# Reordering exponentials, casts and row norms in a hybrid pooling and HGRN2 decoder step

## The chip, the cores and the metric

The kernel runs on the 8 cores of one Trainium2 chip. Each core takes one prompt of 2048 tokens, with the 16 meta tokens ahead of it, and 16 of the 128 sample tokens; no core waits for another. The metric is the device time of the slowest core in microseconds (us), the median of several runs.

## The reference, cut to what matters

```python
h = rmsnorm(x, g_mix)
u, q, f, v, og, ga, gb = split(h @ w_in)      # 4 x 512, 512, then 2 x 1024 columns
# branch A: trailing means over 2, 4, 8, 16 positions, minus the token
ya = (group_map(pool_mean(u) - u) * pool_scale) @ w_a
# branch B: gated linear recurrence, 4 heads, dk = dv = 128
f = lb + (1 - lb) * sigmoid(f);  k = 1 - f
S_t = diag(f_t) S_{t-1} + outer(k_t, v_t);  o_t = S_t^T silu(q_t)
yb = (rmsnorm(o, g_onorm) * silu(og)) @ w_b
x = x + (sigmoid(ga) * ya + sigmoid(gb) * yb) @ w_out
x = x + square(relu(rmsnorm(x, g_mlp) @ w_up)) @ w_down
y = rmsnorm(x, g_final)
```

16 learned meta tokens stand ahead of every prompt and are dropped from y. The last 15 rows of u and the last state S are outputs too.

## The kernel before

The 2048 prompt rows are worked in four groups of 512 (four row tiles of 128). The first stage, `group(g)` for g = 0 to 3, computes everything up to the projection by w_out, with h held transposed (channels on partitions) in `hT[g % 2]`. Group 0 carries the 32 sample and meta rows as well, so its tiles are 544 columns wide where those of the other groups have 512. A tile of 544 columns takes two PSUM banks, one of 512 takes one; `banks` hands out banks 0 to 3 in turn. The second stage, `up(g)` and `down(g)`, is the MLP; the change doesn't touch it.

The order of the work is made by a planner, `Timeline`. `U(fn)` emits a unit, a product that fills one PSUM tile and its eviction, and moves the planner's time t on by 1 (by 0.5 for the products by w_a and w_b, by 2 for the first one by w_out). `tl.at(t, fn)` and `tl.later(dt, fn)` put side work on a list, which is emitted, earliest due time first, after the unit with which t reaches it. Times in the code are thus counted in units, and they set only the place in each engine's queue. Every engine works through its queue in order and waits with semaphores that `Prog` works out from the buffers; DMAs are issued in the queues of SyncE (SP) and of GpSimd (POOL, the weights).

A group runs: four units of f (`u_f`, sigmoid); four of v (`u_v`), four of u (`u_u`) and four of q (`u_q`, silu), in group 0 in that order with a small v unit for the meta and sample rows first, in the others mixed; four of og; then gb, ga with the product by w_a (`u_ya`), the product by w_b (`u_yb`) with the rest of gb; and w_out. ScalarE (ACT) evicts f, v, u, q, og, ga and gb.

Side work, each with its due time counted from `b0`, the end of the f units:

- `prep_ln`, `prep_scan`, `prep_exp`, `prep_k`, `prep_D`, `prep_E`, per head: log of f on ScalarE, running sum on VectorE (DVE), two exponentials on ScalarE (`prep_exp`, which writes one of the two buffers `T3`), the scaled k on VectorE (`prep_k`, which reads `T3`), decay factors. `prep_q(m)` (VectorE) follows each q unit by 1.5.
- `meta_state` (group 0): four transposes of k, their copy by ScalarE, four products into the state, their copy by ScalarE. `state_scale(0)` (VectorE) scales the state, `state_cast` (ScalarE) casts it to bf16 for the products.
- `r_tile(g, t)`: the recurrence on 128 tokens in six steps: `a` (transposes of k and the score product, lines 739 to 749, which read all four heads of k and q), `o` (lines 758 to 765), `n1`, a cast, `n2`, and `p` (transposes of the normed output, then ScalarE's copy into `obT`, which the products by w_b read).
- `pool_u`: running means of each u unit, on VectorE; a scan (line 812) where the window is 8 or 16.
- `rms1` norms one row tile of the next group: ScalarE squares and sums into the bf16 buffer `xn[j]` (two in turn), POOL makes the factor, `scaled` multiplies the rows by it into the same buffer, `fin` transposes them into the next `hT`. `fin` has two forms: eight TensorE transposes and a VectorE eviction that multiplies by g_mix (lines 617 and 572), or, with `dmat`, a DMA transpose issued by SP (line 653), after which `scale_rows` (line 868) multiplies by g_mix in eight VectorE operations for the group. Before, group 0 norms the rows of group 1 in the first form, groups 1 and 2 those of their successors in the second. The rows are loaded into three buffers `xr` in turn, which the residual rows (`xload`, `xslice`) use as well.
- `mk`, `scaled`, `evict`, `warm`: the same norm for group 0's own rows at the start, where `start` (the last argument of `rms1`) puts the multiplication on VectorE, with filler matmuls between.
- `more` (group 0): the blocks of w_in and the other weights, loaded from POOL's queue, where the copies of `prep_exp` stand too (line 686).

## Time and profile before

| what | value |
|---|---|
| median of 3 runs | 917.6 us (917.01 to 918.33) |
| the profiled execution's own time | 917.9 us |
| its span on the slowest core, core 7 | 916.4 us |
| spans of the eight cores | 914.6 to 916.4 us |
| mean granted TensorE clock, core 7 | 0.997 |
| group 0, first matmul of f to that of group 1 | 20.9 to 145.6 us |
| groups 1 and 2 | 145.6 to 249.5 us, 249.5 to 353.4 us |
| group 3 with its last products, then the MLP | to about 458 us, to 916.4 us |

The page counts busy time over the span of one execution. In 40 slices of 22.9 us the busy tenths of TensorE are 9 in all but the first two (4 and 8) and the last (7):

```profile
PE   4889999999999999999999999999999999999997
```

A line of a timeline begins with start and length in us; a group of equal instructions in a row is one line with xN, and the bracket at its end is how long the engine had been idle and which engine and line ended that. Idle time of an engine that nobody waits for costs nothing, so the waits of TensorE are read first.

### The profile page before, as it was taken

The page shows a single profiled execution, that of the slowest core. Times are in us where ns is not written, and L with a number is a line of the kernel's source. Part 1 is how long each engine was busy: PE and PEld are TensorE (multiplying, and loading weights), DVE is VectorE, ACT ScalarE, POOL GpSimd, SP SyncE. Part 2 cuts the span into 40 slices and gives each one's busy share as a digit, 9 for nine tenths or more (in the row PEclk, how much of TensorE's full clock was granted, in tenths as well). Part 3 has the DMA queues.
Part 4 walks back from the last instruction along what each step waited for, and adds up shares of the span by engine and source line. Part 5 has one row for each costly group of instructions (what it writes and reads, how often), then busy time and mean ns, then how long its engine had stood idle before and what let it go on. Part 6 is the DMA issues. An engine that isn't in the chain of part 4 may idle for free.

```text
span 916.4 us, 15069 instructions; the slowest of 8 cores (914.6 to 916.4 us)
## 1 busy us (share of the span) xinstructions
PE 877.8 (96%) x5017; PEld 453.6 (49%) x5017; DVE 419.5 (46%) x692; ACT 360.7 (39%) x636; POOL 120.2 (13%) x190
## 2 busy tenths in 40 slices
PE   4889999999999999999999999999999999999997
PEld 3556654454444444455444444444444444688443
DVE  4654563866657665854543222442143411333122
ACT  4634445566274645552233322332223321333222
POOL 3112330144101530243110000000000000000000
PEclk9999999999999999999999999999999999999999
DMA  9999724138604377996999341300520002200011
GB/s 175 164 169 197 138 79 161 44 107 181 194 28 116 104 173 209 176 140 88 188 210 194 62 125 61 93 1 2 137 70 23 1 20 73 73 1 1 31 64 70
DMA packets 81480, 94.90 MB, mean 104 GB/s; under 512 B 27741, under 2 KB 62173, under 8 KB 81388
## 3 DMA queue, kind: packets, MB, share of 16 engines
q1 hardware_dynamic: 57420, 63.52, 23.8%
q0 software_dynamic: 23984, 30.41, 23.5%
q8 instruction: 42, 0.69, 0.3%
q14 instruction: 34, 0.28, 0.1%
HBM read 92.35 MB, written 26.11 MB: 129 GB/s over the span
## 4 chain that ended last, share of the span: by engine, by line
PE 84%; DVE 5%; ACT 4%; issue 4%; POOL 1%; DMA 1%; DVEq 0%; SPq 0%; ACTq 0%; POOLq 0%
PE ps L591 46%; PE ps L1328 24%; PE ps L603 8%; ACT arena L569 4%; PE ps L1034 2%; DVE arena L572 1%; DVE arena L672 1%; POOL arena L572 1%; DMA arena<-meta 1%; DVE arena L692 0%; PE ps L748 0%; PE ps L1326 0%; PE ps L765 0%; PE ps L617 0%; PE ps L1217 0%
## 5 line engine op out<-in xcount | busy, mean ns | idle before, releaser
L591 PE MATMUL ps<-arena 128*128 128x512 bf16 (+2 forms) x2720 | 494.0, 338 | 10.4 <-ACT arena L569 7.6
L591 PEld LDWEIGHTS ps<-arena 128*128 128x128 bf16 x2720 | 259.8, 98 | 217.0 <-issue 23.6
L569 ACT ACTIVATE arena<-ps 128x512 f32<-128x512 f32 (+7 forms) x328 | 190.8, 598 | 292.4 <-PE ps L591 216.5
L569 ACT ACTIVATE arena<-arena 128x1024 bf16<-128x1024 f32 (+7 forms) x235 | 154.5, 670 | 256.3 <-DVE arena L1342 167.3
L1328 PE MATMUL ps<-arena 128*128 128x512 bf16 x1024 | 222.0, 379 | 0.0
L572 DVE TENSOR_TENSOR arena<-arena 128x512 bf16<-128x512 f32 (+6 forms) x214 | 146.2, 689 | 137.4 <-ACT arena L569 129.0
L1328 PEld LDWEIGHTS ps<-arena 128*128 128x128 bf16 x1024 | 100.0, 98 | 121.4 <-issue 1.3
L572 DVE TENSOR_TENSOR arena<-ps,arena 128x512 f32<-128x512 f32 (+5 forms) x155 | 107.9, 714 | 82.3 <-PE ps L591 26.1
L603 PE MATMUL ps<-arena 128*128 128x512 bf16 (+2 forms) x480 | 109.2, 383 | 0.0
L1342 DVE SCALAR_TENSOR_TENSOR arena<-ps,arena 128x1024 f32<-128x1024 f32 (+2 forms) x18 | 22.0, 1223 | 152.0 <-PE ps L1328 137.4
L572 POOL TENSOR_TENSOR arena<-arena 128x512 f32<-128x512 bf16 (+7 forms) x78 | 75.5, 975 | 73.4 <-DMA arena<-sth 27.1
L603 PEld LDWEIGHTS ps<-arena 128*128 128x128 bf16 (+2 forms) x480 | 46.3, 98 | 57.3 <-issue 3.9
L1351 DVE SCALAR_TENSOR_TENSOR arena<-arena 128x1024 f32<-128x1024 f32 (+2 forms) x18 | 22.0, 1224 | 34.2 <-ACT arena L569 34.2
L672 DVE TENSOR_TENSOR_SCAN arena<-arena 128x512 f32<-128x512 bf16 (+1 forms) x16 | 19.6, 1227 | 22.3 <-ACT arena L569 22.3
L686 POOL COPY arena<-arena 128x4 f32<-128x4 f32 x16 | 7.0, 438 | 96.7 <-ACT arena L569 96.7
L617 PE MATMUL ps<-arena 128*128 128x128 bf16 (+1 forms) x72 | 6.9, 255 | 12.0 <-DVE arena L647 11.0
L868 DVE TENSOR_SCALAR arena<-arena 128x512 bf16<-128x512 bf16 (+1 forms) x48 | 16.8, 350 | 3.1 <-DVE arena L868 0.9
L572 DVE TENSOR_TENSOR ps<-ps,arena 128x512 f32<-128x512 f32 x16 | 11.1, 695 | 10.4 <-PE ps L886 10.4
L752 DVE CAST_PREDICATED arena<-arena,ps 128x512 bf16<-128x512 uint32 x16 | 11.0, 687 | 8.5 <-PE ps L749 8.5
L1034 PE MATMUL ps<-arena 128*128 128x512 bf16 x64 | 14.5, 379 | 0.0
L748 PE MATMUL ps<-arena 128*64 128x128 bf16 x64 | 6.5, 223 | 7.3 <-ACT arena L569 4.5
L617 PEld LDWEIGHTS ps<-arena 128*128 128x128 bf16 (+1 forms) x72 | 5.7, 118 | 14.8 <-issue 14.3
(97 smaller groups left out, 259.2 us busy)
## 6 DMA issues: line engine op xcount, KB each, us to landing
arena<-xp SPq DMA_DIRECT2D x32, 512.0 KB, 5.4
arena<-w_in POOLq DMA_DIRECT2D x9, 1024.0 KB, 20.6
x1d<-arena SPq DMA_DIRECT2D x16, 512.0 KB, 5.2
arena<-w_up POOLq DMA_DIRECT2D x8, 1024.0 KB, 12.8
arena<-x1d SPq DMA_DIRECT2D x16, 512.0 KB, 3.8
y_p<-arena SPq DMA_DIRECT2D x15, 512.0 KB, 2.9
arena<-w_down POOLq DMA_DIRECT2D x5, 1024.0 KB, 23.7
h2d<-arena SPq DMA_DIRECT2D x16, 256.0 KB, 4.9
```

What stands on the lines that cost most here:

```text
L569: P.add("act", lambda h: h.activation(out=out, in_=in_, func=func, **kw), reads=reads, writes=writes)
L572: P.add(eng, lambda h: h.tensor_tensor(out=out, in0=a, in1=b, op=op), reads=reads, writes=writes)
L591: i = h.matmul(ps[:, bb, 0:m], lhsT=wfn(k), rhs=rfn(k, c, m), start=(k == 0), stop=(k == K - 1))
L603: i = h.matmul(ps[0:rows, b, :], lhsT=lfn(k), rhs=rfn(k), start=(k == 0), stop=(k == K - 1))
L617: i = h.transpose(out=o[:, k, 0:rows], in_=src[0:rows, k * 128:(k + 1) * 128], identity=ident_b[0:rows, 0:rows])
L672: P.add("dve", lambda h: h.tensor_tensor_scan(out=t2[:, c:544], data0=smask[:, c - 16:528], data1=t2[:, c:544], initial=0.0, op0=ALU.mult, ...
L752: P.add("dve", lambda h: h.copy_predicated(out=AT[i], mask=tri.bitcast(U32).unsqueeze(1).to_broadcast([128, 4, 128]), data=pA), reads=[b_p ...
L868: P.add("dve", lambda h: h.tensor_scalar(out=X[:, k, 0:n], in0=X[:, k, 0:n], scalar1=w[:, k:k + 1], scalar2=None, op0=ALU.mult), reads=buf ...
L1034: i = h.matmul(ps[:, b + half, :], lhsT=mT[:, k, 0:128], rhs=wo[:, k, half * 512:(half + 1) * 512], start=(k == 0), stop=(k == 7))
L1328: x = h.matmul(ps[0:rows, b + half, :], lhsT=aT[:, f, c:c + rows], rhs=rhs, start=(f == 0), stop=(f == 31))
L1342: P.add("dve", lambda h: h.scalar_tensor_tensor(out=sl, in0=src, scalar=s_(2), in1=sl, op0=ALU.mult, op1=ALU.add), reads=bsrc + [bst] + bx ...
L1351: P.add("dve", lambda h, c0=c0, c1=c1: h.scalar_tensor_tensor(out=xi[0:rows, c0:c1], in0=xi[0:rows, c0:c1], scalar=s_(5), in1=gfin[0:rows, ...
```

## The change

It touches the planner's due times and one form, not the arithmetic apart from where g_mix is multiplied in for group 1:

- `prep_exp` and `prep_k` of group 0 go from due times 2, 3, 4, 6 after `b0` to 2, 4, 6, 7 (the planner's e = 1 is in these), `prep_E` to 8; those of the other groups stay.
- `meta_state` is cut in two; the product and its copy come 1.1 later.
- the first `state_cast` of each group goes from 10 to 13.2 after `b0` (2 more in group 0).
- pooling of u units 2 and 3 of group 0: due 1.4 to 1.9 later.
- rows of group 1: normed in group 0 from due time 10 after the og units rather than 12, transposed by DMA, scaled by `scale_rows`; in all groups `scaled` comes 2.4 after the square rather than 1.6, `fin` 3.6 after it rather than 3.1. Row loads move with them.
- start: row tile 2 is multiplied on VectorE rather than ScalarE, and after the eviction of tile 1.

```diff
@@ -711,13 +711,15 @@
             tt(E, D1, D2[:, :, 0:4], ALU.mult, [b_D1, b_D2], [b_E])
             P.add("dve", lambda h: h.tensor_copy(out=D2[:, :, 0:1], in_=D2[:, :, 4:5]), reads=[b_D2], writes=[b_D2])
 
-        def meta_state():
+        def meta_1():
             def tr(h):
                 for k in range(4):
                     i = h.transpose(out=psT[0:32, k, :], in_=kt[:, k, 0:32], identity=ident_b)
                 return i
             P.add("pe", tr, reads=r_kt.bufs + [b_idb], writes=[b_pT[0]])
             act(ktT[1][0:32], psT[0:32, 0:4, :], AF.Copy, [b_pT[0]], r_ktT[1].bufs)
+
+        def meta_2():
 
             def mu(h):
                 for k in range(4):
@@ -818,7 +820,7 @@
                 if g == 0:
                     P.add("dve", lambda h: h.tensor_copy(out=u_s[:, gg, :], in_=u[:, 0:16]), reads=bu, writes=[b_us])
                 P.add("dve", lambda h: h.tensor_copy(out=hist[:, gg, :], in_=u[:, 528:544]), reads=bu, writes=[b_hist])
-            a, b = (((5.0, 5.0), (4.6, 4.6), (5.1, 6.1), (6.2, 7.2)) if g == 0 else ((4.9, 4.9), (3.4, 3.5), (5.5, 6.5), (4.6, 5.6)))[gg]
+            a, b = (((5.0, 5.0), (4.6, 4.6), (7.0, 8.0), (7.6, 8.6)) if g == 0 else ((4.9, 4.9), (3.4, 3.5), (5.5, 6.5), (4.6, 5.6)))[gg]
             for op in first + mid:
                 tl.later(a, op)
             tl.later(b, fin)
@@ -1065,7 +1067,7 @@
                 early = {}
                 A(19.5, load_rest2)
                 for t in range(3):
-                    A(20.1 + t, lambda t=t: ([activate(r) for r in r_x[1:3]] if t == 0 else None, early.update({t: xload(x_rows(1, t), 128, r_wa.bufs)})))
+                    A(21.1 + 0.3 * t, lambda t=t: ([activate(r) for r in r_x[1:3]] if t == 0 else None, early.update({t: xload(x_rows(1, t), 128, r_wa.bufs)})))
                 A(24.1, lambda: [fold_wa2(gg) for gg in range(4)])
                 A(27.0, sample_pool)
                 A(36.0, fold_wb)
@@ -1100,17 +1102,19 @@
             def B(t, fn):
                 tl.at(b0 + t, fn)
             e = 1 if g == 0 else 0
+            x0_, x1_, x2_, x3_ = (2, 4, 6, 7) if g == 0 else (1, 2, 3, 5)
             B(0, lambda: ([prep_ln(g, i) for i in range(4)], prep_scan(g, 0), prep_scan(g, 1)))
-            B(1 + e, lambda: (prep_exp(g, 0), prep_scan(g, 2), prep_k(g, 0)))
-            B(2 + e, lambda: (prep_exp(g, 1), prep_scan(g, 3), prep_k(g, 1)))
-            B(3 + e, lambda: (prep_exp(g, 2), prep_k(g, 2)))
-            B(5 + e, lambda: (prep_exp(g, 3), prep_k(g, 3), prep_D(g)))
-            B(6 + e, lambda: prep_E(g))
+            B(x0_, lambda: (prep_exp(g, 0), prep_scan(g, 2), prep_k(g, 0)))
+            B(x1_, lambda: (prep_exp(g, 1), prep_scan(g, 3), prep_k(g, 1)))
+            B(x2_, lambda: (prep_exp(g, 2), prep_k(g, 2)))
+            B(x3_, lambda: (prep_exp(g, 3), prep_k(g, 3), prep_D(g)))
+            B(x3_ + 1, lambda: prep_E(g))
             e = 2 if g == 0 else 0
             if g == 0:
-                B(9, meta_state)
+                B(9, meta_1)
+                B(10.1, meta_2)
             B(9 + e, lambda: ([activate(r) for r in r_sogr], state_scale(0)))
-            B(10 + e, state_cast)
+            B(13.2 + e, state_cast)
             rs = [r_tile(g, t) for t in range(4)]
             for t in range(4):
                 z = 15.6 + e + 3.35 * t
@@ -1141,18 +1145,17 @@
 
                 def pre(t):
                     i = xl[t]
-                    rfin.append(rms1(xr[i], r_x[i].bufs, 128, t, N[:, :, 128 * t:128 * t + 128], bN[t], g > 0))
-                for t, z in enumerate((0, 1, 2, 14 if g == 0 else 9)):
+                    rfin.append(rms1(xr[i], r_x[i].bufs, 128, t, N[:, :, 128 * t:128 * t + 128], bN[t], True))
+                for t, z in enumerate((0, 1, 2, 13 if g == 0 else 9.5)):
                     if g > 0 or t == 3:
                         tl.later(z, lambda t=t: xl.update({t: xload(x_rows(g + 1, t), 128)}))
-                for t, z in enumerate((12, 16, 19, 22) if g == 0 else (7, 11, 14, 17)):
+                for t, z in enumerate((10, 13, 16, 19) if g == 0 else (7, 11, 14, 17)):
                     tl.later(z, lambda t=t: pre(t))
-                    tl.later(z + 1.6, lambda t=t: rfin[t][0]())
-                    tl.later(z + 3.1, lambda t=t: (activate(r_hT[(g + 1) % 2]) if t == 0 else None, rfin[t][1]()))
-                if g > 0:
-                    for k in range(8):
-                        tl.later(24.2 + 0.6 * k, lambda k=k: scale_rows(N, bN[0:4], gmix, k, 512))
-            for t, z in enumerate((18, 21, 24) if g == 0 else (13, 16, 19)):
+                    tl.later(z + 2.4, lambda t=t: rfin[t][0]())
+                    tl.later(z + 3.6, lambda t=t: (activate(r_hT[(g + 1) % 2]) if t == 0 else None, rfin[t][1]()))
+                for k in range(8):
+                    tl.later(24.2 + 0.6 * k, lambda k=k: scale_rows(N, bN[0:4], gmix, k, 512))
+            for t, z in enumerate((16, 19, 22) if g == 0 else (13.5, 16.5, 19.5)):
                 tl.later(z, lambda t=t: xi.update({t: xslice(xload(x_rows(g, t), 128))}))
             for m in range(4):
                 U(lambda: u_gb(m))
@@ -1208,7 +1211,7 @@
         def mk(t):
             if t < 0:
                 return rms1(xr[i_sp], r_x[i_sp].bufs + [b_meta], 32, 4, hT[0][:, :, 0:32], r_hT[0].bufs[4], False, None, True)
-            return rms1(x0[t], r_x0[t].bufs, 128, t, hT[0][:, :, 32 + 128 * t:160 + 128 * t], r_hT[0].bufs[t], False, (xn0[t], r_xn0[t].bufs[0]), t < 2)
+            return rms1(x0[t], r_x0[t].bufs, 128, t, hT[0][:, :, 32 + 128 * t:160 + 128 * t], r_hT[0].bufs[t], False, (xn0[t], r_xn0[t].bufs[0]), t < 3)
 
         def warm(n):
 
@@ -1227,9 +1230,9 @@
         evict[0]()
         warm(2)
         scaled[-1]()
-        scaled[2]()
         evict[1]()
         warm(2)
+        scaled[2]()
         scaled[3]()
         evict[-1]()
         evict[2]()
```

## Rows read from the trace of the kernel before

**Rows 1.** The page: busy time per engine, and three of the costliest groups
```profile
PE 877.8 (96%) x5017; PEld 453.6 (49%) x5017; DVE 419.5 (46%) x692; ACT 360.7 (39%) x636; POOL 120.2 (13%) x190
...
L569 ACT ACTIVATE arena<-ps 128x512 f32<-128x512 f32 (+7 forms) x328 | 190.8, 598 | 292.4 <-PE ps L591 216.5
...
L572 DVE TENSOR_TENSOR arena<-arena 128x512 bf16<-128x512 f32 (+6 forms) x214 | 146.2, 689 | 137.4 <-ACT arena L569 129.0
...
L868 DVE TENSOR_SCALAR arena<-arena 128x512 bf16<-128x512 bf16 (+1 forms) x48 | 16.8, 350 | 3.1 <-DVE arena L868 0.9
```

**Rows 2.** The timeline, 36 to 50 us: start, length, engine, operation, [idle before]
```profile
36.74 1.37 ACT L569 ACTIVATE arena<-arena 128x528 f32<-128x528 f32 x2 [0.72 <-DVE arena L572]
...
38.74 2.01 PE L591 MATMUL ps<-arena 128*128 128x272 bf16 x16 [1.42 <-ACT arena L569]
...
40.00 1.37 ACT L569 ACTIVATE arena<-arena 128x528 f32<-128x528 f32 x2 [1.40 <-DVE arena L692]
...
41.99 5.72 PE L591 MATMUL ps<-arena 128*128 128x272 bf16 x48 [1.24 <-ACT arena L569]
...
42.40 1.44 DVE L692 SCALAR_TENSOR_TENSOR arena<-arena 128x528 bf16<-128x528 f32 x2
...
49.05 0.38 PE L724 MATMUL ps<-arena 32*128 32x128 bf16 x4 [1.01 <-ACT arena L569]
```

**Rows 3.** The timeline, group 0, 51 to 72 us, to the first score product
```profile
51.47 1.28 ACT L569 ACT_TABLE_LOAD   x1 [1.34 <-PE ps L591]
...
58.95 0.63 ACT L569 ACTIVATE arena<-arena 128x512 bf16<-128x512 f32 x1 [2.68 <-DVE arena L944]
...
63.15 0.68 DVE L572 TENSOR_TENSOR arena<-arena 128x512 bf16<-128x512 f32 x1
...
64.08 0.22 PE L748 MATMUL ps<-arena 128*64 128x128 bf16 x1 [2.80 <-DVE arena L811]
...
64.40 7.04 PE L603 MATMUL ps<-arena 128*128 128x512 bf16 x24
```

**Rows 4.** The windows behind that wait: busy time, granted clock (PEclk), DMA
```profile
64.08:66.50 2.42, 2.42 (x14) 1.09 (x15) 2.42 (x5) 0.00 (x0) 0.00 (x0) 0.61 1.10 168
```

**Rows 5.** The timeline, group 1, 174 to 178 us, to the first score product
```profile
174.50 0.63 ACT L569 ACTIVATE arena<-arena 128x512 bf16<-128x512 f32 x1 [3.39 <-DVE arena L572]
...
176.21 0.69 DVE L572 TENSOR_TENSOR arena<-arena 128x512 bf16<-128x512 f32 x1 [1.20 <-ACT arena L569]
...
177.16 0.22 PE L748 MATMUL ps<-arena 128*64 128x128 bf16 x1 [1.50 <-ACT arena L569]
```

**Rows 6.** The timeline, 214 to 225 us: norms of group 2
```profile
214.77 1.15 ACT L569 ACTIVATE arena<-arena 128x1024 bf16<-128x1024 f32 x1 [1.52 <-POOL arena L572]
...
216.55 1.89 PE L591 MATMUL ps<-arena 128*128 128x512 bf16 x8 [0.91 <-ACT arena L569]
...
224.45 1.06 ACT L569 ACTIVATE arena<-arena 128x1024 bf16<-128x1024 f32 x1 [0.45 <-DMA arena<-arena]
```

**Rows 7.** Line 653: the eight DMA transposes of groups 1 and 2
```profile
DMA to landing us min/median/max: 3.3/4.5/7.4
```

**Rows 8.** The timeline, 112 to 146 us: TensorE, transposes of group 1
```profile
112.93 0.61 PE L617 MATMUL ps<-arena 128*128 128x128 bf16 x8
...
123.70 5.59 PE L591 MATMUL ps<-arena 128*128 128x272 bf16 x40 [0.84 <-DVE arena L572]
...
135.21 10.52 PE L603 MATMUL ps<-arena 128*128 128x512 bf16 x48
```

**Rows 9.** The timeline, 14 to 17 us: DVE and TensorE before the first group
```profile
14.46 1.54 DVE L572 TENSOR_TENSOR arena<-ps,arena 128x1024 bf16<-128x1024 bf16 x2
...
16.02 1.01 PE L617 MATMUL ps<-arena 128*128 128x128 bf16 x8 [0.93 <-ACT arena L569]
```

**Rows 10.** The q block of w_in: issue (timeline), time to landing
```profile
19.39 0.88 POOL L503 DMA_DIRECT2D arena<-w_in  x1 [2.00 <-issue]
...
arena<-w_in POOLq DMA_DIRECT2D x1, 1024.0 KB, 22.4
```

## Prediction

> **What bounds the kernel now.** I read the page first: TensorE is busy for 878 of the 916 us, VectorE for 420 and ScalarE for 361 [rows 1]. So only two things change the time: work taken from TensorE's queue, and its waits. The next view is therefore the timeline of TensorE alone, filtered for lines with a wait, and for each wait the timelines of ScalarE and VectorE just before it, to see what was queued ahead of the instruction waited for. The MLP has next to no such wait; the change can gain in the first 458 us only.
>
> In group 0 the u units wait twice, 1.42 and 1.24 us, for v's evictions, which stand behind exponentials that wait for VectorE; the meta product waits 1.01 us [rows 2]. The longest wait is 2.80 us before the first score product [rows 3]: it needs `prep_q(3)`, which sits on VectorE behind the pooling of u unit 2 and late because ScalarE waited 2.68 us at the state cast. After it the granted clock falls to 0.61 [rows 4] and 24 matmuls take 7.04 us [rows 3], where at full clock 48 take 10.52 [rows 8]. Groups 1 to 3 have one pattern each (one stands for three): ScalarE waits 3.39 us at the cast, the last q eviction and `prep_q` are late, and TensorE waits 1.50 us [rows 5]. Groups 1 and 2 lose 0.91 us more behind a `scaled` that waits for POOL [rows 6].
>
> **Part 1, exponentials, casts and pooling in group 0.** I redo the order by hand. A unit of 544 columns takes 5.72 / 3 = 1.9 us [rows 2], one of 8 matmuls 10.52 / 6 = 1.75 [rows 8], an eviction 0.6 [rows 1], a pair of exponentials 1.37 [rows 2]. The v units end at 38.74 - 1.42 = 37.3 [rows 2]. With v2's eviction ahead of the second exponential pair (36.74 to 38.1), u0 starts at 37.3 and u1, u2, u3 follow to 44.9. The next late thing is the fourth exponential: it needs the k of head 1, which VectorE ends at 42.40 + 0.72 = 43.1 as before [rows 2]. ScalarE then runs 43.2 to 44.7 (with `prep_D`'s small one) and evicts u2 to 45.3, which q0's banks wait for. So q0 starts at 45.4 instead of 49.05 + 0.38 = 49.4 [rows 2]. The waits of 1.42, 1.24 and 1.01 are gone and about 0.4 comes back. What hides the moved exponentials is the u units; POOL's small copies behind them move along, and the loads in POOL's queue come out earlier, not later. Four q units and the meta product (now between q1 and q2, its copy made under q1) reach 45.4 + 7.6 + 0.2 = 53.2; two og units and the transposes, 56.9. VectorE starts its q work when q0 is evicted: 47.3, plus the table load of 1.28 [rows 3], plus 0.6 = 49.2. Ahead of the score product it then has ten large operations of 0.69 [rows 1], 6.9 us: 56.1. The upper bound is the measured stretch, first q eviction (51.47 + 1.28 + 0.6 = 53.4) to the end of `prep_q(3)` (63.8), 10.4 us [rows 3], which would be 59.6; but this contains the scan, the addition and the final operation of u2 and the waits for the cast, all of which move behind it. I take 57.1, near the lower end: 64.08 - 57.1 = 7.0 us won, 4.5 at the other bound. Without a wait of 2.8 us the clock should stay up: 7.04 - 24 x 0.219 = 1.8 us [rows 3, 8], 0 if it falls all the same. The cast itself, moved behind og1, costs 0.63 on an idle ScalarE; its readers, the o products, come 2 units later. Queued behind VectorE's moved pooling are the copy of scores and two folds, wanted two units on: nothing.
>
> **Part 2, the cast in groups 1 to 3.** The transposes ahead of the wait end at 177.16 - 1.50 = 175.66; VectorE is free at 176.21 - 1.20 = 175.01 [rows 5] and ends `prep_q(3)` at 175.7 if q3 was evicted on time, so about 0.15 of the wait stays: 1.35 won, three times, 4.05 us (bounds 3.0 and 4.5).
>
> **Part 3, rows of group 1 by DMA.** Removed are four times eight transposes. By columns each set is 8 x 128 / 512 x 0.219 = 0.44 us of TensorE (0.61 with the modelled end), 1.8 in all, and the 0.84 us wait for their eviction [rows 8]. Added are four DMA transposes on SP, 3.3 to 7.4 us to landing, median 4.5 [rows 7], and eight scalings of 0.35 [rows 1], 2.8 us of VectorE, during the products by w_out (8 x 1.75 = 14 us), where VectorE has eight additions of 0.69, 5.5 us [rows 1]: hidden; uncovered they would cost 2.8. Behind the transposes in SP's queue are residual rows that are wanted units later. But the new due times put work on ScalarE ahead of evictions, in a stretch where a 544-column ga tile takes both banks of its pair and the next may not start before the last is evicted. After ga5 ScalarE has eviction, obT copy, `scaled` and the square, 0.6 + 0.6 + 1.15 + 1.06 [rows 1, 6] = 3.4 us, against 3.0 us of TensorE (transposes 0.22, a w_a product 0.88, ga6 1.9): 0.45 lost. After ga7 `scaled` of tile 1 (1.15) now stands ahead of the last obT copy, which the product by w_b needs: 1.15 lost. Net -1.8 - 0.84 + 1.6 = -1.0 (bounds -2.6, if other slack takes both, and +2, if two squares also wait 1.5 us each for a landing).
>
> The Trainium skill (VectorE: DVE Perf Modes, The three transpose paths) gives 390 ns for a 128 x 128 bf16 transpose on TensorE and 1309 ns by DMA, and advises TensorE wherever PSUM may be the target. By that each row tile of eight blocks would be an estimated 7.4 us slower by DMA, and the four 29 us if they lay on the path. The landings above say that they needn't; it is the rival on the slow side below.
>
> **Part 4, `scaled` later in groups 1 and 2.** ScalarE waited 1.52 us for POOL, TensorE 0.91 [rows 6]; behind ga6's eviction this wait disappears. But the transpose of tile 1 is then issued one place later on SP, behind a sample store, while the square of tile 3, which reuses its `xn`, already waited 0.45 for the landing [rows 6]; the gb eviction behind it comes up to 1.5 late. Bounds per group -0.9 and +0.9; I take -0.3, so -0.6.
>
> **Part 5, start.** The ScalarE wait of 0.93 before tile 2's transposes [rows 9] is replaced by VectorE's order: eviction of tile 1 (14.46, at most 1.54 with a small one), then the multiplication, twice 0.35 [rows 1] or more: 15.7 + 0.75 + 0.1 = 16.5 instead of 16.02 [rows 9]. I take +0.45 (0 to +1); everything behind shifts.
>
> **Sum.** -7.0 - 1.8 - 4.05 - 1.0 - 0.6 + 0.45 = -14.0. The profiled execution took 917.9, hence 903.9; the median is 0.3 lower: 903.6.
>
> **The rivals.**
>
> A, new waits on ScalarE for landings. For it: the 0.45 of rows 6, and a landing of 7.4 [rows 7]. A square in group 0 (two of them) and one each in groups 1 and 2 wait up to 7.4 - 4.5 = 2.9 us longer, half of it hidden: 4 x 1.5 = 6, thus 909.6. Against it: in group 0 no sample traffic competes.
>
> B, VectorE is what is late next in group 0. The score product then comes at 59.6, not 57.1, and the clock falls again: 2.5 + 1.8 = 4.3, thus 907.9. Against it: the ten counted operations.
>
> C, weights. The q block, issued at 19.39, lands 22.4 us later, at 41.8 [rows 10]; q0 now wants it at 45.4, not 49.4. A slip over 3.6 us eats the gain one for one; the DMA share of 1.10 behind it [rows 4] shows that the engines are full, so one block's delay reaches the next. A loss of 3 gives 906.6.
>
> D, slower than before: DMA transposes that land as late as a weight block in the loaded stretch, 22.4 us [rows 10]. The square of tile 2 stands about 5 us behind the issue of tile 0's transpose and would hold ScalarE, and all evictions behind it, for 22.4 - 5 = 17.4 us: 903.6 + 17.4 = 921.0. It decides from a landing of about 5 + 14 = 19 us in group 0. Against it: the eight landings of rows 7, and w_out is the only weight still loading then.
>
> E, the moves leave the queues' waits where they are (another operation is late in each case): 917.6.
>
> **How the numbers follow.** Forecast 903.6 with 0.67 (899.5 to 907 alone), A 0.14, B 0.08, C 0.04, D 0.03, E 0.04. The lower end is the sum with each part at its good bound (part 1 -7.3, clock -1.8, casts -4.5, part 3 -2.6, part 4 -1.8, start 0: -18.0, 899.6). The upper end takes in A, 910. Outside are D, E and A's worse half at one side, about 0.14, and 0.04 below. A measurement of this kernel can tell about 0.2% (1.8 us) from no change: faster 0.94, same 0.03 (most of E), slower 0.03 (D).
>
> **What would show each step.** Part 1: no wait of TensorE over 0.5 us before the u units, q0 near 45.4 (plus the start's shift), first score product near 57.5, a granted clock of 1.00 after it. Part 2: in groups 1 to 3 a wait under 0.3 us there, no ScalarE wait at a cast. Part 3: no line 617 behind the start; waits of about 0.5 and 1.2 us after ga5 and ga7 for ScalarE; group 1's f units straight behind w_out's products. Part 4: no 0.91, a wait for a DMA at the fourth square. Part 5: tile 2's transposes near 16.5. The prediction is wrong if group 0 is shorter by less than 7 us or groups 1 and 2 are not shorter by 1 us each.

## The result, and the profile after

The changed kernel takes 910.6 us (median of six runs) where the kernel before takes 918.0 on the same chip: a ratio of 0.9915, with a 95% interval of 0.9899 to 0.9931. A second measurement, `f1_changed` below, gave 0.9923. The medians count executions in which the cores of one die were granted a lower clock (two of the six, over 1018 us, and one of those before); without these they are 909.7 and 917.8 us, and all ratios here leave such executions out. So it is 7 to 8 us faster, not 14: 910.6 lies 0.6 us above the end of the forecast range, 910, and 909.7 just inside it. Its profiled execution took 909.6 us, with a span of 908.1 on the slowest core, core 2. The ratios below are all to the kernel before on the same chip; 0.001 is 0.9 us, and each interval reaches 0.0009 to 0.0016 to either side.

The timeline of the changed kernel first, core 2, for the stretches of [rows 2] and [rows 3] (start, length, engine, line, operation, [idle before and what ended it]):

```profile
36.83 7.58 PE L591 MATMUL ps<-arena 128*128 128x272 bf16 x64
...
44.67 3.88 PE L591 MATMUL ps<-arena 128*128 128x272 bf16 x32
...
46.78 1.28 ACT L569 ACT_TABLE_LOAD   x1 [1.18 <-PE ps L591]
...
56.52 0.24 PE L750 MATMUL ps<-arena 128*64 128x128 bf16 x1
```

The four u units now run in one piece of 64 matmuls with no wait, q0 starts at 44.67, and the score product comes at 56.52 with no wait, where it came at 64.08 behind 2.80 us. The window behind it answers to [rows 4] (us; busy time of PE, PEld, DVE, ACT, POOL; granted clock; DMA share; GB/s):

```profile
56.50:59.00 2.50, 2.50 (x20) 1.25 (x19) 2.50 (x6) 1.19 (x3) 0.76 (x1) 1.00 1.11 178
```

The clock is 1.00, not 0.61. Twenty microseconds on, the same timeline shows a wait of TensorE that the kernel before did not have:

```profile
63.65 1.47 SPq L496 DMA_DIRECT2D arena<-xp  x3
...
69.51 0.87 POOL L503 DMA_DIRECT2D arena<-w_b  x1
...
70.54 0.59 PE L864 MATMUL ps<-arena 128*128 128x512 bf16 x2 [0.49 <-ACT arena L569]
...
76.28 4.87 DVE L866 CAST arena<-ps 128x512 bf16<-128x512 f32 x8 [9.57 <-DMA arena<-xp]
77.11 2.38 PE L864 MATMUL ps<-arena 128*128 128x512 bf16 x4 [5.98 <-DVE arena L866]
...
80.57 3.45 PE L591 MATMUL ps<-arena 128*128 128x272 bf16 x16
```

Line 866 copies the folded w_a (group map and pool scale multiplied in, `fold_wa2`) back over w_a. The three early row loads of group 1 are emitted ahead of it and list w_a's buffer among what they read, `xload(x_rows(1, t), 128, r_wa.bufs)`. That holds them until w_a has landed, at 63.3; and it also holds whoever overwrites w_a until they have landed. The view of these loads gives their landing:

```profile
DMA to landing us min/median/max: 8.0/9.8/11.4
```

The last, issued at 64.7, lands at about 76. VectorE stands still for 9.57 us and TensorE for 5.98 (3.5 to 6.0 on the eight cores). The windows say what this does to the clock:

```profile
71.00:77.00 6.00, 0.13 (x1) 0.00 (x0) 0.72 (x2) 0.00 (x0) 0.00 (x0) 0.69 1.07 239
77.10:84.00 6.90, 6.85 (x35) 4.06 (x36) 5.94 (x10) 0.60 (x1) 0.00 (x0) 0.54 1.08 144
84.00:90.00 6.00, 5.59 (x56) 4.59 (x55) 1.97 (x6) 2.84 (x5) 2.00 (x5) 1.00 1.12 169
```

For 6.9 us behind the wait TensorE has 0.54 of its clock, most of it at the 1.2 GHz level: 16 matmuls take 3.45 us, against 2.01 at 84.94. In the kernel before, on core 7, the last of these loads was issued at 67.2 and landed 12.1 us later, at 79.3, and the fold's copy began 0.1 us behind that:

```profile
79.44 4.87 DVE L864 CAST arena<-ps 128x512 bf16<-128x512 f32 x8 [3.52 <-PE ps L862]
```

There was next to no slack, and on core 2 of that execution the copy already waited 4.58 us, for the loads, instead of 3.52. Whatever brings the fold forward further than the landing therefore turns into a wait. The fold's third product comes 9.2 us earlier than before (70.54 against 79.77), which would put the copy at 70.2, and the last load landed at 76.1: 5.9 us, the wait that was measured. By 83.9 us only 1.3 of the 9.2 us are left. Of the 7.9 us lost 5.98 are the wait, so some 2 us are the price of the low clock (an estimate; the expectations below say 2.2).

The first score product of group 1 and the cast ahead of it [rows 5], and the norms of group 2 [rows 6]:

```profile
172.81 1.08 ACT L569 ACTIVATE arena<-ps 128x512 bf16<-128x512 f32 x2 [1.24 <-PE ps L603]
...
173.04 0.22 PE L750 MATMUL ps<-arena 128*64 128x128 bf16 x1 [0.21 <-DVE arena L572]
...
215.22 1.15 ACT L569 ACTIVATE arena<-arena 128x1024 bf16<-128x1024 f32 x1
215.58 2.75 PE L591 MATMUL ps<-arena 128*128 128x512 bf16 x12 [0.93 <-ACT arena L569]
```

The wait at the score product is 0.21, not 1.50 (0.21 and 0.56 in groups 2 and 3, 1.50 in both before). The wait of 0.91 is gone. One of 0.66 at the first `u_yb` has grown to 0.93. Then the rows of group 1 [rows 8] and the start [rows 9]:

```profile
109.83 2.01 PE L591 MATMUL ps<-arena 128*128 128x272 bf16 x16 [0.20 <-ACT arena L569]
...
112.63 1.14 ACT L569 ACTIVATE arena<-arena 128x1024 bf16<-128x1024 f32 x1
...
113.67 0.59 ACT L569 ACTIVATE arena<-ps 128x512 bf16<-128x512 bf16 x1
...
114.40 3.74 PE L591 MATMUL ps<-arena 128*128 128x512 bf16 x24 [1.47 <-ACT arena L569]
114.69 1.06 ACT L569 ACTIVATE arena<-arena 128x1024 bf16<-128x1024 f32 x1 [0.43 <-DMA arena<-arena]
```

```profile
14.34 1.21 DVE L572 TENSOR_TENSOR arena<-ps,arena 128x1024 bf16<-128x1024 bf16 x1
...
16.35 0.61 PE L617 MATMUL ps<-arena 128*128 128x128 bf16 x8 [1.39 <-DVE arena L647]
```

The second half of group 0, from the end of gb3 (83.85) to the first f unit of group 1 (142.75), is 58.90 us against 60.45. From its own first f unit group 0 is 122.9 us long against 124.7, so 1.8 us shorter, not the 7 us under which the prediction called itself wrong; groups 1 and 2 are 2.1 and 2.4 us shorter.

### The profile page after: what moved, and what is told of

It reads as the page before. It is cut to its first block, busy times and chain, and to the rows that moved or that the text cites. A ratio compares the mean times of both kernels' runs of the same rounds, so it can differ in the third digit from the quotient of the medians.

```text
span 908.1 us, 14934 instructions; the slowest of 8 cores (903.9 to 908.1 us)
## 1 busy us (share of the span) xinstructions
PE 868.5 (96%) x4904; PEld 451.7 (50%) x4985; DVE 418.1 (46%) x697; ACT 359.4 (40%) x635; POOL 121.1 (13%) x190
## 4 chain that ended last, share of the span: by engine, by line
PE 85%; DMA 4%; ACT 4%; issue 3%; DVE 3%; POOL 0%; SPq 0%; DVEq 0%; ACTq 0%; POOLq 0%
PE ps L591 47%; PE ps L1331 24%; PE ps L603 8%; ACT arena L569 3%; DMA arena<-xp 2%; PE ps L1036 1%; DMA arena<-w_in 1%; DVE arena L572 1%; DVE arena L672 1%; PE ps L888 0%; PE ps L767 0%; PE ps L1329 0%; PE ps L750 0%; PE ps L625 0%; PE ps L762 0%
## 5 line engine op out<-in xcount | busy, mean ns | idle before, releaser
L591 PE MATMUL ps<-arena 128*128 128x512 bf16 (+2 forms) x2678 | 490.3, 338 | 9.3 <-ACT arena L569 5.5
L569 ACT ACTIVATE arena<-arena 128x1024 bf16<-128x1024 f32 (+6 forms) x234 | 152.4, 666 | 241.2 <-DVE arena L1345 168.9
L572 DVE TENSOR_TENSOR arena<-ps,arena 128x512 f32<-128x512 f32 (+5 forms) x151 | 103.6, 701 | 75.5 <-PE ps L591 27.6
L603 PE MATMUL ps<-arena 128*128 128x512 bf16 (+2 forms) x468 | 106.2, 379 | 1.8 <-DMA arena<-w_in 0.6
L870 DVE TENSOR_SCALAR arena<-arena 128x512 bf16<-128x512 bf16 (+1 forms) x56 | 19.6, 349 | 2.9
L617 PE MATMUL ps<-arena 128*128 128x128 bf16 (+1 forms) x40 | 3.6, 246 | 12.5 <-DVE arena L647 12.4
L814 DVE TENSOR_TENSOR_SCAN arena<-arena 128x512 f32<-128x512 f32 x8 | 11.7, 1462 | 0.9
## 6 DMA issues: line engine op xcount, KB each, us to landing
arena<-w_in POOLq DMA_DIRECT2D x9, 1024.0 KB, 21.2
```

Of the source, the lines that this page charges most:

```text
L569: P.add("act", lambda h: h.activation(out=out, in_=in_, func=func, **kw), reads=reads, writes=writes)
L572: P.add(eng, lambda h: h.tensor_tensor(out=out, in0=a, in1=b, op=op), reads=reads, writes=writes)
L591: i = h.matmul(ps[:, bb, 0:m], lhsT=wfn(k), rhs=rfn(k, c, m), start=(k == 0), stop=(k == K - 1))
L603: i = h.matmul(ps[0:rows, b, :], lhsT=lfn(k), rhs=rfn(k), start=(k == 0), stop=(k == K - 1))
L814: mid.append(lambda: P.add("dve", lambda h: h.tensor_tensor_scan(out=d1[:, 16:528], data0=u[:, 32:544], data1=u[:, 32 - w:544 - w], initia ...
L870: P.add("dve", lambda h: h.tensor_scalar(out=X[:, k, 0:n], in0=X[:, k, 0:n], scalar1=w[:, k:k + 1], scalar2=None, op0=ALU.mult), reads=buf ...
```

## The experiments

Two theories after the traces. W: the fold waits for the row loads, and through them for w_a's landing, and this wait took the gain. F: the DMA engines are nearly full until about 110 us (share 0.83 to 1.13 in windows of 5 and 6 us from 84 on), so that without this wait the next transfer is late.

**Without the listed reads.**

```diff
-early.update({t: xload(x_rows(1, t), 128, r_wa.bufs)})
+early.update({t: xload(x_rows(1, t), 128)})
```

> The changed kernel, but the three early row loads of group 1 no longer carry w_a's buffers among their reads, which only ordered them behind w_a's load; nothing is left out. Theory W (the loads hold w_a: as long as they read its buffers in the program's book-keeping, VectorE may not write the folded w_a until they land): the wait of 3.5 to 6.0 us in the products of line 864 goes on every core, and the low clock behind it (2.2 us on the slowest core); 902 to 904. Rival F (the DMA engines are full there, and the next thing that TensorE needs from them, block ga0 or the rows, comes as late): the wait moves to another line, 908 to 911.

Measured 0.9939 (0.9926 to 0.9952), 913.3 us: outside both expectations, and no faster than the changed kernel (1.5 to 2.2 us slower, with intervals that overlap). The wait of the fold is gone, and the ga unit that began at 103.72 begins 7.6 us earlier, at 96.12. The fold's copy no longer waits for the loads, though these are still under way (the last, issued at 63.6, lands 11.2 us later, at 74.8): it was the listing of the buffer that held it.

```profile
70.58 4.87 DVE L866 CAST arena<-ps 128x512 bf16<-128x512 f32 x8 [3.31 <-PE ps L864]
```

Then this, on core 5 (5.1 to 8.8 us on the eight cores):

```profile
101.22 2.46 SPq L653 DMA_TRANSPOSE arena<-arena  x1
...
106.65 6.23 SPq L653 DMA_TRANSPOSE arena<-arena  x1
...
117.54 1.06 ACT L569 ACTIVATE arena<-arena 128x1024 bf16<-128x1024 f32 x1 [10.88 <-DMA arena<-arena]
...
119.35 1.07 PE L591 MATMUL ps<-arena 128*128 128x272 bf16 x4 [8.80 <-ACT arena L569]
```

The square of row tile 2 writes the `xn` that tile 0's DMA transpose reads. The view of line 653 for this stretch:

```profile
L653 SPq DMA_TRANSPOSE arena<-arena x4: 1216/1838/6234, 101.2 to 129.8; - x4
...
DMA to landing us min/median/max: 5.1/9.0/16.2
```

101.2 + 16.2 = 117.4: the square starts as that transpose lands. This is the prediction's rival D by its own mechanism. Of theory F the general part came, a late transfer behind the wait that was removed, but neither of the two that it named.

The same edit on the kernel before:

> The kernel before with the same edit alone. Theory W: the loads land at about 78.2 us and the fold comes at 78.7, so nothing waited for them on most cores: within 0.15% of the kernel before, 917 to 918.5. If the reads of w_a had cost something before as well, or if loads issued before w_a's landing delay weights: over 1.5 us away from it.

Measured 0.9994 (0.9985 to 1.0003). The listed reads cost nothing there; they came to cost with part 1.

The edit of `e1_free`, and the loads due behind the fold (`A(25.1 + 0.3 * t, ...)` for `A(21.1 + 0.3 * t, ...)`):

> The changed kernel without those reads and with the three row loads due 25.1 to 25.7 instead of 21.1 to 21.7, so behind the fold. Theory W: as the kernel without the reads, within 1 us (902 to 904). If the loads' traffic delays block ga0 (rival F), this one is faster than the kernel without the reads by 1 us or more, and the wait before ga0 is shorter.

Measured 0.9943, as `e1_free` but again far from the 902 to 904 us expected, with a wait of 7.10 us in the same place as there. The loads as such are not what matters.

**Is it the transposes, and is it the weights?** Three variants of `e1_free`: rows of group 1 by TensorE as before (`e5_tensor_rows`); four normed tiles, in the buffers `xn0` of the start (`e9_own_xn`); half of w_out not loaded and the other half used twice (`e7_half_wout`).

```diff
-rfin.append(rms1(xr[i], ..., bN[t], True))
+rfin.append(rms1(xr[i], ..., bN[t], g > 0))                                            # e5
+rfin.append(rms1(xr[i], ..., bN[t], True, (xn0[t], r_xn0[t].bufs[0]) if g == 0 else None))   # e9
-for k in range(8):
+for k in range(8 if g > 0 else 0):                                                     # e5
```

> The kernel of e1 (the changed kernel, early row loads listing no buffer of w_a), and group 1's rows transposed by TensorE as before the change, so no DMA transpose in group 0. Theory L (in e1 a DMA transpose that lands late among the weight blocks holds xn, and through it the square and the evictions): the wait of 5.1 to 8.8 us before tile 0's products by w_b goes, none over 1.5 us takes its place, and TensorE does some 1.8 us more work: 901.5 to 905. Rival Q (ScalarE's queue of squares, copies and evictions is itself too long in this stretch, the landing only happened to end last): a wait for ScalarE of 3 us or more stays in the second half of group 0 and the time is 908 to 912.

Measured 0.9878 (0.9865 to 0.9892), 907.4 us, 2.4 above the expected range. The longest wait in the second half is 1.84 us, where 1.5 was expected. Theory L holds; the extra is told under part 3.

> The kernel of e1, but the norm of group 1's rows writes four normed tiles of its own instead of two in turn, so that no square waits for a transpose to land; the four DMA transposes stay. Theory L: landings stay up to 16 us, no ScalarE wait for one, no TensorE wait over 1.5 us in the second half of group 0, unless the last landing reaches the f units of group 1 (then up to 3 us there): 900.5 to 904.5. Rival Q: a wait for ScalarE of 3 us or more stays: 908 to 912.

Measured 0.9840 (0.9826 to 0.9853), 903.9 us. The same stretch:

```profile
107.40 4.82 SPq L653 DMA_TRANSPOSE arena<-arena  x1
107.55 12.62 PE L591 MATMUL ps<-arena 128*128 128x512 bf16 x85 [1.46 <-ACT arena L569]
```

and its view of line 653:

```profile
L653 SPq DMA_TRANSPOSE arena<-arena x4: 1215/2208/4824, 102.0 to 119.3; - x4
...
DMA to landing us min/median/max: 5.7/8.0/11.9
```

The transposes are still late, and nobody waits for them: TensorE's products run through.

> The kernel of e1, loading only rows 0 to 511 of w_out and using them twice, so that half of that weight's bytes are not moved (a part of the computation is changed). Theory T (the transposes land late because w_b and w_out load beside them): the longest landing falls from 16 to under 11 us, the wait of 8.8 us to under 4, time 904 to 909. Rival S (the landing is late because of the order in SP's queue or the transposes' own pace): landing, wait and time as in e1, 912 to 914.5.

Measured 0.9845 (0.9831 to 0.9858), at the good end. The landings, with the same two `xn`:

```profile
DMA to landing us min/median/max: 5.9/6.6/7.3
```

ScalarE waits 1.9 us for one and TensorE not at all. So theory T: w_out's transfer beside them makes the transposes late. In `e1_free` it was issued at 85.84 and took 30.9 us, into the transposes; in the changed kernel it was issued at 93.44 and took 17.5, and they landed in 4.8 to 6.5. The first transpose is issued 15.4 us behind w_out in both (101.22, 108.82). What differs is what moves beside w_out: w_b landed 14.9 us behind w_out's issue in `e1_free`, at 100.8, and 2.9 behind it in the changed kernel (issued at 69.51, landed 26.8 us later, at 96.3), where it had moved on while TensorE waited for the fold. That this alone makes w_out's transfer 13 us shorter is read from the rows and was not run by itself.

The rows of group 1 by TensorE in the changed kernel itself (the lines of `e5_tensor_rows`, with the listed reads):

> The changed kernel with group 1's rows transposed by TensorE as before; the wait of the fold of w_a stays. The prediction put the DMA transposes at -1.0 us (bounds -2.6 to +2), so this run should be 911 to 913.5, 911.6 by its sum. If the wait for the fold and the new waits after ga5 and ga7 have eaten that part (1.47 us after ga7), it is 909 to 910.6.

Measured 0.9963 (0.9951 to 0.9976), 915.4 us: outside both expectations, 3.7 to 4.4 us slower than the changed kernel, not 1.0.

The four normed tiles in the changed kernel, the listed reads kept:

> The changed kernel with the four normed tiles of e9, while the early row loads still list w_a's buffer. Theory L (two bounds one behind the other, both set by what the DMA engines still carry): the wait of the fold of w_a stays at 4 to 8 us, and the own tiles bring nothing, because w_out is issued and landed that much earlier relative to the transposes: 910.5 to 912.5, as the changed kernel. Rival: the normed tiles alone hold some of the loss of the changed kernel: 907 to 910.

Measured 0.9939 (0.9927 to 0.9952), 913.2 us, 0.7 above the expected range, with the fold's wait of 7.51 us and landings of 4.5 to 5.9. The normed tiles bring nothing as long as the fold waits: the two bounds stand one behind the other, and neither edit alone (`e1_free`, `g1_own_xn_reads`) gains, both together 7 us.

**The parts, each undone in the kernel of `e9_own_xn`** (0.9840), where nothing behind takes a gain back. The changed kernel itself:

> The changed kernel as it is, beside its variants on the same chip. Against the kernel of e9 (903.9 there) it should be 6 to 8 us slower, 910 to 912: 6.0 for the wait of the fold of w_a, some 2.2 for the clock behind it, less what is given back.

Measured 0.9923 (0.9909 to 0.9937), 912.5 us: 7.6 us slower than `e9_own_xn`.

```diff
-x0_, x1_, x2_, x3_ = (2, 4, 6, 7) if g == 0 else (1, 2, 3, 5)
+x0_, x1_, x2_, x3_ = (2, 3, 4, 6) if g == 0 else (1, 2, 3, 5)
-(7.0, 8.0), (7.6, 8.6)
+(5.1, 6.1), (6.2, 7.2)
```

> The kernel of e9 with the exponentials (2, 3, 4, 6) and the pooling of u units 2 and 3 of group 0 where they were before the change; meta product, casts and the rest stay moved. The prediction's part 1 put this at 7.0 us and 1.8 of clock; the traces of before and after said 7.6 and a clock that stays at 1.00. If these moves alone give it and nothing behind takes it back in this kernel: 903.9 + 7 to 9.4, 911 to 913.3, with a wait of 1 to 2.8 us at the score product of group 0. Rival: in this kernel too something behind has slack for it (weights that are late anyway), or the cast and the meta product, which stay moved, were half of it: 906 to 909.

Measured 0.9893 (0.9877 to 0.9909), 4.9 us slower and between the two expectations. The old waits are back, but not all of them:

```profile
39.31 2.01 PE L591 MATMUL ps<-arena 128*128 128x272 bf16 x16 [1.43 <-ACT arena L569]
42.57 5.72 PE L591 MATMUL ps<-arena 128*128 128x272 bf16 x48 [1.25 <-ACT arena L569]
...
62.47 0.22 PE L750 MATMUL ps<-arena 128*64 128x128 bf16 x1 [1.99 <-DVE arena L813]
```

and the window behind, columns as above:

```profile
62.40:64.90 2.50, 2.44 (x18) 1.24 (x19) 2.50 (x5) 0.12 (x1) 0.00 (x0) 1.00 1.16 156
```

The wait at the score product is 1.99, not 2.80, and the clock stays at 1.00 behind it. From the first f unit to the score product this kernel takes 41.0 us (core 5), `e9_own_xn` 36.4 (core 1) and the kernel before 43.2: the exponentials and the pooling are 4.6, the cast and the meta product, which stayed moved here, the other 2.2.

State cast back, `B(10 + e, state_cast)` for `B(13.2 + e, state_cast)`, on `e1_free` and on `e9_own_xn`:

> The changed kernel without the reads, and the first state cast of each group back at due time 10 instead of 13.2. By my sum the cast is worth 1.35 us in each of groups 1 to 3 (4.05), and about nothing to 2.7 us in group 0, where it stands before the eviction of the last q unit: slower than the kernel without the reads by 4 to 6.5 us, 906 to 910, and a wait of TensorE of about 1.5 us before the first score product of groups 1 to 3. Rival: the cast's wait is hidden by other work once the exponentials are spread, under 2 us.

> The kernel of e9 with the state cast ten units into each group (twelve in group 0), as before the change. The prediction's part 2: 1.35 us for each of groups 1 to 3, 4.05, and in group 0 the cast was part of the wait at the score product (0.6 in the trace of e4): 903.9 + 4.05 + 0.6 = 908.5, with waits of 1.5 at the score products of groups 1 to 3. Rival (given back at yb0, where the later cast makes the wait 0.93 instead of 0.66, or elsewhere): under 907.

Measured 0.9973 (3.1 us over `e1_free`, less than expected: group 1 begins no later, at 145.2 us against 146.5 on the slowest cores and 1.0 earlier in the mean of all eight, so that the cast's part of group 0 was absorbed by the wait for the transpose) and 0.9888 (0.9875 to 0.9902; 4.4 us over `e9_own_xn`). The waits are back as the forecast had them, 0.61 in group 0 and 1.51, 1.50 and 1.51 in groups 1 to 3:

```profile
167.97 0.22 PE L750 MATMUL ps<-arena 128*64 128x128 bf16 x1 [1.51 <-ACT arena L569]
```

The start's order back (`scaled[2]()` ahead of `evict[1]()`, last argument of `rms1` `t < 2`), twice:

> The kernel of e9 with the start's order as before the change (tile 2's scaling on ScalarE ahead of tile 1's eviction). The prediction put the new order at +0.45 (0 to +1), which gives 903.4; the profiled core of after had its f units 1.0 us earlier than that of before, thanks to a full clock, which would give 904.9. Both are near what five rounds can tell; the row that tells is the start of group 0's f units and the granted clock of tile 2's transposes on all cores.

> The kernel of e9 with the start's order of before, a second time, beside the next kernel: 902.6 as in its first run, within 0.7.

Measured 0.9819 (0.9805 to 0.9833), 902.6 us, and 0.9835 (0.9822 to 0.9848), 903.5 us, against 0.9840. The times alone don't settle it: the two lie 1.9 and 0.5 us under `e9_own_xn`, and the intervals overlap. The rows of all traces of this case say more. The mean over the eight cores of the first f unit's start is 20.6 to 21.2 us in twelve of the thirteen traces with the new order and 20.1 in the other, the first one of the changed kernel; it is 20.0 to 20.3 in four of the five with the old order and 20.7 in the other (`f3b_start_back`). The means are 20.8 and 20.2: by these the new order costs about 0.6 us, which fits the sign of the times.

Scaling and transposes of groups 1 and 2 due as before (`z + 1.6`, `z + 3.1` where g > 0):

> The kernel of e9 with the scalings and transposes of groups 1 and 2 due 1.6 and 3.1 units behind the square, as before the change. The prediction put the new times at -0.3 for each group, -0.6 in all: 904.5. The traces left -0.8 for each group behind the cast's part: 905.5. The wait of 0.91 at a ga unit should be back in both groups, and the wait at yb0 fall from 0.93 to 0.66.

Measured 0.9854 (0.9840 to 0.9868), 1.3 us slower, within the intervals, which overlap. Of the two expected signs one came: the wait of 0.91 of [rows 6] is back, while that at the first `u_yb` stays at 0.93, which the later cast alone must have made (it is 0.66 in `f5_casts_back`).

Last, on `f3_start_back`, `scaled` and, in the same way, `fin` (4.2 for 3.6) of group 1's tile 1 due 0.6 later:

```diff
-tl.later(z + 2.4, lambda t=t: rfin[t][0]())
+tl.later(z + (3.0 if g == 0 and t == 1 else 2.4), lambda t=t: rfin[t][0]())
```

> The kernel before it, with the scaling of group 1's tile 1 (1.14 us on ScalarE) and its transpose due 0.6 later, behind the copy of obT that the product by w_b wants. The prediction put 1.15 us of the wait after ga7 down to this scaling; the wait was 1.46. If that is right, 0.3 of it stays and the time is 1.15 shorter, 901.4. Rival (the transpose, then later, holds something, or the wait is the copy's own way through ScalarE): no change.

```profile
106.36 14.70 PE L591 MATMUL ps<-arena 128*128 128x512 bf16 x95 [0.43 <-ACT arena L569]
```

The wait of 1.47 is 0.43: its 1.04 were the moved scaling's, as forecast. On the clock it is 0.9825 (0.9812 to 0.9838) against 0.9835 for the kernel without the edit beside it, within the intervals: the row settles the mechanism, the times don't settle the gain. These kernels of about 903 us are some 15 us faster than the kernel before and some 8 faster than the changed one.

## Why the prediction was right and wrong

**Part 1: right where it looked, and it didn't look far enough.** u0 to u3 in one piece, q0 at 44.67 (45.4 forecast, with a start 1.0 earlier than in the trace of before instead of 0.45 later), so 24.8 us behind the first f unit where the forecast makes it 24.5; score product 36.6 us behind it where the forecast makes it 36.2; no table-load or eviction wait beyond those counted, clock 1.00. The step that failed is the sentence at its end: behind VectorE's moved pooling were "two folds, wanted two units on: nothing". The fold was costed as queue work on VectorE and not by what it waits for. Its overwrite of w_a waits for three loads that were emitted ahead of it, and these wait for w_a. They hardly move when the fold comes 9.2 us earlier: issue at 63.3 to 67.2 before, 63.65 to 64.7 after, the last landing at 79.3 before and at 76.1 after. The rule of the prediction's own first part, to name for each earlier step what is late next, was applied to evictions and weights and not to this buffer; the forecast puts this wait, and the clock behind it, at nothing. Its price on core 2 was 5.98 of wait and some 2 of clock, 8 us (of the 9.2 gained at the fold's third product 1.3 are left at 83.9); between `e9_own_xn` and the two measurements of the changed kernel lie 6.9 and 7.6. `e1_free` shows the cause (the wait goes with the listed reads), `e2_before_free` that it was new, `g1_own_xn_reads` that it is the first of two.

**The sum.** Without both late transfers the changed order takes 903.9 us in `e9_own_xn`, and 0.9840 is 14.7 us; the sum was 14.0. That they agree so closely is in part luck, as the terms' errors go both ways. They are, in us:

| part | forecast | trace | undone on the chip |
|---|---|---|---|
| 1, to the score product | -7.0 | -6.5 from the first f unit | 4.9 exponentials and pooling alone |
| 1, clock behind it | -1.8 | 1.00 instead of 0.61 | not separately |
| 2, casts | -4.05 | -1.29 in groups 1 and 2, -0.94 in group 3 | 4.4, 0.6 of it in group 0 |
| 3, rows of group 1 by DMA | -1.0 | -1.55 in its half of group 0 | 3.5 (`e5` against `e9`) |
| 4, `scaled` later | -0.6 | -0.8 in group 1, -1.1 in group 2 | 1.3, within the intervals |
| 5, start | +0.45 | +0.6 in the mean of 18 traces | +0.5 and +1.9, within the intervals |

**Part 2** was right in mechanism, and nearly in size: 3.5 us by the rows for 4.05, since in group 3 a wait of 0.56 stays where under 0.3 was forecast.

**Part 3** was under-sized. Of the two new waits one is right: 1.47 for the 1.15 after ga7 (the copy behind the scaling adds 0.3). After ga5, where 0.45 was forecast, it is 0.20, but the kernel before had 0.17 at the same unit (111.08), so this one is hardly new; that the total, 1.67, is near the 1.6 forecast is luck. What was too small is what it saves. In `e5_tensor_rows` the TensorE form, at the new due times, waits 1.84 + 0.23 + 0.18 = 2.25 us, where the kernel before waited 0.84 + 0.17: 1.78 of transposes (four times 0.445) + 2.25 - 1.67 = 2.4 us, which is what the rows of the two traces differ by in this half (27.61 against 25.21 us, from the ga unit that waits 0.45 to the first product by w_out); the time says 3.5, with intervals that reach 1.2 to either side. So part of the 3.5 is the price of the TensorE form at due times made for the other one, and -1.55 is the nearer measure of the change itself (1.78 + 0.84 + 0.17 - 1.67 = 1.1 of it by the waits that are listed; where the rest lies they don't show).

**Rival D** was priced nearly right and judged too unlikely. It put the square "about 5 us behind the issue of tile 0's transpose"; in `e1_free` ScalarE was free for it 5.4 behind, and a landing of 16.2 us, under the 19 from which it was to decide, took 8.8 us from TensorE. Against it stood that "w_out is the only weight still loading then". This was so (w_b landed at 100.8, just ahead of the transpose), and that one 2 MB block was enough, as `e7_half_wout` shows. In the changed kernel itself D did not happen (ScalarE waits 0.43 us on core 2, up to 1.7 on the others), because w_out's transfer, 13 us shorter there, ended at 110.9, 2 us behind the issue of the first transpose.

The advice that the prediction weighed (the Trainium skill, VectorE: DVE Perf Modes, Rules for kernel authors: TensorE wherever PSUM may be the target) comes out both ways in these runs. With two `xn` tiles the TensorE form is 5.6 us faster (0.9878 against 0.9939), with four it is 3.5 slower (0.9878 against 0.9840). What decides here is whether anyone waits for the landing.

**Rivals A, B, C, E.** A priced the kernel at 909.6 us, within 1 us of the first measurement, but this is luck: ScalarE waits 0.43 us for a landing in group 0 and 0.63 in groups 1 and 2 together on core 2 (at most 1.7 and 3.0 on any core), and the loss came from the fold, which A doesn't name. No VectorE wait at the score product of group 0 (B). No wait for the q block (C; it landed at about 42.6, 2 us ahead of its use), though the first v unit waited 0.64 us for its block (28.09), over the 0.5 of the listed sign; one core of the kernel before waited 1.10 there. All moved waits went (E).

**Part 4** was sized at 0.3 us for each group; group 1 is 2.10 us shorter in all (101.75 against 103.85), 0.8 more than the cast's 1.29, group 2 2.4 (101.48 against 103.85), 1.1 more, and the time says 1.3 for both, within the intervals. The term taken off for the fourth square's wait was too large: in groups 1 and 2 together ScalarE waits for such a landing once, 0.63 us. **Part 5**: tile 2's transposes came where forecast, but in the profiled core ran at full clock (0.61 us against the 1.01 of [rows 9]), so that its f units began 1.0 earlier; over its eight cores they begin at 19.2 to 21.4 us, against 19.2 to 20.9 before. A start on one core, or in one trace, is no measure at this size; over 18 traces it is 0.6 later, near the 0.45 forecast.

## What to carry to other kernels

When a change brings an engine forward, list for the next 30 us every instruction that overwrites a buffer and every transfer still in flight, and read off how much slack each had: here the gain ended at the smallest slack, and behind it stood the next. A buffer listed as read only to order a transfer also holds whoever writes that buffer until the transfer has landed. Where DMAs free buffers that are used in turn, one buffer for each DMA in flight took the landing off the path here; otherwise the landing has to be costed at what the queues carry then, not at its median elsewhere.

## What the hardware showed unexpectedly

- A DMA transpose of 128x1024 bf16 lands in 4.8 to 6.5 us in this stretch of the changed kernel, in 5.1 to 16.2 with w_out's 2 MB beside it, and its issue on SP's queue takes 1.2 to 1.4 us in one case and up to 6.23 in the other. With half of w_out left out it is 5.9 to 7.3, and 1.2 to 2.2 on SP.
- The clock behind a wait: 0.54 behind 5.98 us and 0.61 behind 2.80, but 1.00 behind 1.99 at the same place in `f2_group0_back`. The lost clock was worth an estimated 2 and 1.8 us. No run here shows what decides between the two cases.
- w_out, issued at 93.44, landed 17.5 us later in the changed kernel (110.9); issued at 85.84 in `e1_free` it took 30.9 us (116.7). In `g1_own_xn_reads` (95.40) it took 18.1 and in `e9_own_xn` (86.60) 26.3. Issued 7.6 us earlier in `e1_free`, it landed 5.8 us later than in the changed kernel, on the cores shown.
